# Recurrence stage: where the dense products stand between the levels, and who makes the exclusive sums

## The reference, cut to what matters

```python
def hgrn2_direction(q, i, z, lb, qc, ic, zc, ctx_out, reverse):
    kc, lfc = forget_terms(zc, lb)
    ...
    k, lf = forget_terms(z, lb)
    o, _ = hgrn2_scan(flip(q), flip(k), flip(i), flip(lf), s_ctx, True)
    ...
step (per chunk):
    scores = jnp.einsum('bhcd,bhsd,bhcsd->bhcs', q_n, k_n, w)
    o_n = o_inter + jnp.einsum('bhcs,bhse->bhce', scores, v_n)
    return d_n[..., None] * s + jnp.einsum('bhcd,bhce->bhde', ks_n, v_n), o_n
```

## Time and profile before

| | before |
|---|---|
| median of the runs (3) | 2460.62 us |
| lowest, highest | 2453.39 us, 2463.84 us |
| the profiled execution | 2457.86 us, span 2456.1 us |
| TensorE busy in the span | 2243.3 us (91%) |
| VectorE, GpSimd, ScalarE busy | 1104.9 us, 835.7 us, 668.0 us |
| mean granted TensorE clock | 0.948 |

### The profile page before, as it was taken

How to read it: one execution, slowest core, us unless ns; L and a number is a source line. 1 busy time by engine, 2 the same in 40 slices (tenths; PEclk the granted TensorE clock), 3 DMA queues, 4 the chain that set the end, 5 groups by cost and what they waited for, 6 DMA issues and landing times. The chain is left out here.

```text
span 2456.1 us, 27907 instructions
## 1 busy us (share of the span) xinstructions
PE 2243.3 (91%) x11655; PEld 1798.7 (73%) x11655; DVE 1104.9 (45%) x1647; ACT 668.0 (27%) x1030; POOL 835.7 (34%) x393
## 2 busy tenths in 40 slices
PE   5989996978999999999798878999998999999998
PEld 3768885856676767787665667888887767888886
DVE  2023557652556556556996553111116783111113
ACT  3222223223444444453111333010003163010111
POOL 1322102410323323223800024554554345454553
PEclk7999997979999999999899988999999999999999
DMA  9321115351101011112121012332322222232322
GB/s 296 83 72 52 35 35 172 79 163 52 35 23 47 18 35 35 35 52 78 42 65 35 35 35 70 102 103 86 103 92 97 86 86 69 86 103 88 101 95 77
DMA packets 173212, 187.45 MB, mean 76 GB/s; under 512 B 25552, under 2 KB 151840, under 8 KB 172960
## 3 DMA queue, kind: packets, MB, share of 16 engines
q1 hardware_dynamic: 165520, 178.56, 23.1%
q10 hardware_dynamic: 6992, 5.01, 0.7%
q0 software_dynamic: 576, 2.10, 0.2%
HBM read 183.56 MB, written 2.10 MB: 76 GB/s over the span
## 5 line engine op out<-in xcount | busy, mean ns | idle before, releaser
L2816 POOL TENSOR_TENSOR weights_lo<-weights_raw,weights_hi 128x2048 fp32r<-128x2048 f32 (+1 forms) x104 | 471.0, 4528 | 849.5 <-ACT weights_hi L1334 637.6
L646 PE MATMUL ring<-input_hi,weights_hi 128*128 128x512 f32 x784 | 305.4, 390 | 0.0
L648 PE MATMUL ring<-input_hi,weights_lo 128*128 128x512 f32 x784 | 305.0, 389 | 0.0
L647 PE MATMUL ring<-input_lo,weights_hi 128*128 128x512 f32 x784 | 305.0, 389 | 0.0
L2653 DVE CAST weights_hi<-weights_raw 128x2048 fp32r<-128x2048 f32 (+1 forms) x72 | 88.8, 1233 | 378.6 <-PE ring L648 173.9
L2807 POOL TENSOR_TENSOR h_w<-h_p 128x512 f32<-128x512 f32 x56 | 70.3, 1256 | 448.1 <-PE ring L935 367.6
L908 PE MATMUL obank<-acts,weights_raw 128*128 128x512 f32 x384 | 175.2, 611 | 0.8 <-issue 0.8
L646 PEld LDWEIGHTS ring<-input_hi,weights_hi 128*128 128x128 f32 x784 | 147.2, 188 | 31.1 <-issue 0.5
L648 PEld LDWEIGHTS ring<-input_hi,weights_lo 128*128 128x128 f32 x784 | 147.2, 188 | 30.6
L647 PEld LDWEIGHTS ring<-input_lo,weights_hi 128*128 128x128 f32 x784 | 147.2, 188 | 30.5 <-issue 0.2
L919 PE MATMUL obank<-weights_raw,acts 128*128 128x256 f32 x640 | 145.4, 387 | 0.0
(11 more groups left out here) (457 smaller groups left out, 4459.2 us busy)
## 6 DMA issues: line engine op xcount, KB each, us to landing
weights_raw<-in_w_ada SPq DMA_DIRECT2D x24, 1024.0 KB, 7.2
weights_raw<-in_ffn_w_gate SPq DMA_DIRECT2D x22, 1024.0 KB, 5.2
weights_raw<-in_ffn_w_up SPq DMA_DIRECT2D x22, 1024.0 KB, 5.2
weights_raw<-in_w_in_c SPq DMA_DIRECT2D x20, 1024.0 KB, 5.1
weights_raw<-in_ffn_w_down SPq DMA_DIRECT2D x16, 1024.0 KB, 4.9
weights_raw<-in_w_in_ab SPq DMA_DIRECT2D x9, 1024.0 KB, 5.2
weights_raw<-in_ev_w_in SPq DMA_DIRECT2D x8, 1024.0 KB, 5.8
weights_raw<-in_od_w_in SPq DMA_DIRECT2D x8, 1024.0 KB, 5.8
```

The costliest lines, as they stand in the source:

```text
L646: pe.matmul(o, hi[:, k, ms], xh[:, k, t0:t0 + n], start=k == 0, stop=False)
L647: pe.matmul(o, hi[:, k, ms], xl[:, k, t0:t0 + n], start=False, stop=False)
L648: last = pe.matmul(o, lo[:, k, ms], xh[:, k, t0:t0 + n], start=False, stop=k == KD - 1)
L2816: pool.tensor_tensor(W_LO[slot][:, 0:kt, :], WR[:, slot, 0:kt, :], w_hi[:, 0:kt, :], ALU.subtract).then_inc(sem("w_lo"), 1)
```

## The change

There are four edits.

1. `c_slots`: units of the dense product are put behind other levels. Steps with five units (0, 2, 4) now have them behind levels 0, 1, 2, 4 and in a place 7 behind level 6; steps with six (1, 3, 5, 6) behind 0, 1, 2, 3, 5 and in place 7. Step 7 is as before. ScalarE's evictions move along.
2. For backward steps the scans start at the second token and add the neighbour's term, which gives sums without the token's own term. The chunk sums add that term back (12 elements). GpSimd's `exclusive` and ScalarE's wait for it are gone. Two small fills of the first column are new, in the preparation of step 1 alone.
3. The query's part of `state_operands` becomes `query_operand`, behind `level_scores(st, 0)` and the previous pair's `inside`, ahead of `states`.
4. Ahead of step 0, `state_factors(0)` and the first two level exponentials stand in front of ScalarE's evictions of the second and third i unit.

```diff
@@ c_slots
-            return units + [None] * (8 - len(units))
+            places = range(8) if st == LAST else (0, 1, 2, 4, 7) if len(units) == 5 else (0, 1, 2, 3, 5, 7)
+            placed = dict(zip(places, units))
+            return [placed.get(i) for i in range(8)]
@@ ScalarE, state_factors
                 if d:
-                    act.wait_ge(sem("hg_excl"), STEPS[st][0] + 1)
                     act.activation(HZ[b][:, :, :], HP[b][:, :, :], ACT.Exp)
@@ ScalarE, ahead of step 0
-            for part in range(3):
-                take_product(("i", 0, part))
+            take_product(("i", 0, 0))
             state_factors(0)
             level_exp(0)
             level_exp(1)
+            take_product(("i", 0, 1))
+            take_product(("i", 0, 2))
@@ VectorE, log_f_and_sums, backward steps
+                    for h in range(HH):
+                        dve.tensor_tensor_scan(HP[b][:, h, 1:L], HT_[b][:, h, 0:L - 1], tab("chunk", 1, L), 0.0, ALU.add, ALU.mult)
+                        last = dve.tensor_tensor_scan(HP[b][:, h, L + 1:LT], HT_[b][:, h, L:LT - 1], tab("chunk", 1, LC), 0.0, ALU.add, ALU.mult)
+                    link(last)
+                    link(dve.tensor_tensor(PL[b], ends[0], ends[1], ALU.add))
@@ VectorE
             def state_operands(st):
...
+            def query_operand(st):
+
+                b, q = st % 2, STEPS[st][0] % 2
                 dve.wait_ge(*product_emptied(("q", STEPS[st][0], 1)))
                 dve.tensor_tensor(HT_[b][:, :, 0:L], HT_[b][:, :, 0:L], HQ[q][:, :, :], ALU.mult).then_inc(sem("hg_qi"), 1)
@@ GpSimd
-            def exclusive(st):
-
-                b, d = st % 2, STEPS[st][1]
-                if d == 1:
-                    pool.wait_ge(sem("hg_sums"), st + 1)
-                    pool.tensor_tensor(HP[b][:, :, :], HP[b][:, :, :], HT_[b][:, :, :], ALU.subtract).then_inc(sem("hg_excl"), 1)
```

More of the change, by code:

```diff
@@ L2113, in log_f_and_sums @@
                 dve.wait_ge(sem("hg_lf"), st + 1)
[L2114 to L2118, removed]
+                ends = [v[:, :, :].rearrange("p h (c t) -> p h c t", t=P)[:, :, :, P - 1] for v in (HP[b], HT_[b])]
+                if STEPS[st][1] == 0:
+                    for h in range(HH):
+                        dve.tensor_tensor_scan(HP[b][:, h, 0:L], tab("chunk"), HT_[b][:, h, 0:L], 0.0, ALU.mult, ALU.add)
+                        last = dve.tensor_tensor_scan(HP[b][:, h, L:LT], tab("chunk", 0, LC), HT_[b][:, h, L:LT], 0.0, ALU.mult, ALU.add)
+                    link(last)
+                    link(dve.tensor_copy(PL[b], ends[0]))
+                else:
+                    if st == 1:
+                        dve.memset(HP[b][:, :, 0:1], 0.0)
+                        link(dve.memset(HP[b][:, :, L:L + 1], 0.0))
+                    for h in range(HH):
+                        dve.tensor_tensor_scan(HP[b][:, h, 1:L], HT_[b][:, h, 0:L - 1], tab("chunk", 1, L), 0.0, ALU.add, ALU.mult)
+                        last = dve.tensor_tensor_scan(HP[b][:, h, L + 1:LT], HT_[b][:, h, L:LT - 1], tab("chunk", 1, LC), 0.0, ALU.add, ALU.mult)
+                    link(last)
+                    link(dve.tensor_tensor(PL[b], ends[0], ends[1], ALU.add))
                 dve.tensor_copy(DEC[b], PL[b]).then_inc(sem("hg_sums"), 1)
             def state_operands(st):
-                b, q = st % 2, STEPS[st][0] % 2
+                b = st % 2
                 dve.wait_ge(sem("hg_k"), st + 1)
@@ L2251, in _ @@
                 more = st + 1 < len(STEPS)
+                dve.wait_ge(*product_emptied(("q", hb, 1)))
                 level_operand(7 * st)
@@ L2257, in _ @@
                     inside(hb - 1)
+                query_operand(st)
                 states(st)
@@ L2787, in _ @@
         def _(pool):
-            def exclusive(st):
-                b, d = st % 2, STEPS[st][1]
-                if d == 1:
-                    pool.wait_ge(sem("hg_sums"), st + 1)
-                    pool.tensor_tensor(HP[b][:, :, :], HP[b][:, :, :], HT_[b][:, :, :], ALU.subtract).then_inc(sem("hg_excl"), 1)
-                    pool.wait_ge(sem("hg_excl"), STEPS[st][0] + 1)
             def level_args(g):
@@ L2845, in _ @@
                     if more:
-                        exclusive(st + 1)
                         pool.wait_ge(sem("hg_sums"), st + 2)
```

## The result

The changed kernel takes 2465.58 us (median of 20 runs, 2463.21 to 2468.83) against 2459.59 us before (20 runs, 2451.96 to 2463.84): ratio 1.0033, interval 1.0026 to 1.0041. It is 6 us slower; 2467 was forecast. The profiled execution took 2463.21 us, its span 2461.4.

A forecast was written before the change was run, and what follows sets the result against it. TensorE was taken to bound the kernel, through its idle time and clock. Steps 0 to 6 gave +17.4 us, the start -8.9, step 7 -1.7: together +6.8, forecast 2467 us, range 2450 to 2482.

The forecast's parts named there:

- The start: Step 0: with factors made ahead of two evictions, level 0 starts at about 604.3 instead of 613.18, -8.9 us.
- The step ends: Seven step ends: with a unit behind level 6, level 0 waits about 0.4 us instead of 1.65 to 2.1.
- Level 4 in even steps: Steps 0, 2, 4: without the unit before it, TensorE waits 4.5 us for the operand, three times, 13.5 us.
- Level 5 in odd steps and step 6: Without the unit before it, TensorE waits 5.85 us for the operand, four times, 23.4 us.
- The clock: Behind each of the seven new waits TensorE's low clock costs d = 3.0 us, bounds 0 and 5.0.
- Rivals B: Waits as worked out, but the clock hardly falls, 0 to 1.7 us per wait: 2451 to 2458 us; chance 0.18.
- C: Long low-clock stretches behind the waits at levels 4 and 5, 5 us each: 2481 us; chance 0.14.
- Rival D: Step-end waits shrink, but the clock still falls at all seven, 1.8 us each: 2480 us; chance 0.09.
- The rule of the Trainium skill: Transposes don't count as busy for the clock, so turned keys would still lower it at step ends; weighed against the forecast.
- Edit 2: Level 5's operand without GpSimd's subtraction: second half 0.69 us instead of 3.91; the wait would be hidden without edit 1.
- Edit 3: Query's operand moved ahead of the states and level 2's operand: worth nothing, both ways; 1.2 us in three steps if open.
- Rival E: VectorE's chain to the levels' operands gets shorter, 1.7 us in each of seven steps: 2446 us; chance 0.09.

The follow-up runs named there:

- the start alone: Edit 4 alone on the kernel before (first factors and exponentials ahead of two evictions): 2450.22 us, ratio 0.9969.
- the fillers: Changed kernel with 4 filler matmuls ahead of level 4 and 6 ahead of level 5 at the seven waits: 2452.98 us, ratio to before 0.9973.
- the old places: Changed kernel with the dense product's units back where they stood before (edits 2, 3 and 4): 2439.92 us, ratio to before 0.9929.
- the sums alone: Edit 2 alone on the kernel before (exclusive sums by the scan, no subtraction on GpSimd): 2459.68 us, ratio 1.0008.
- the query back: Changed kernel with the query's operand back in its old place (edits 1, 2, 4): 2467.13 us, ratio to before 1.0034.

## Why the prediction was right, point by point

**The start**, -8.9: level 0 at 604.48 instead of 613.18, -8.7. Right, and confirmed by the start alone.

**The step ends**, seven of 0.4 us: 0.32 each.

**Level 4 in even steps**, 4.5 us: 4.34, three times. **Level 5 in odd steps and step 6**, 5.85 us: 5.83 three times and 6.13 in step 6. The sum of the seven, 36.9 us: 36.6. (The numbers given for the odd steps, 724.6 - 718.66, make 5.9 and not 5.85, which is 0.3 us in all.) Both came out of one comparison: where TensorE could be without the unit, and when VectorE's operand is ready in the trace of before.

**The clock**, d = 3.0 us: 472.86 us of the seven steps (level 0 at 604.48 to level 0 at 1077.34), less 411.3 of work, 36.6 and 2.3 of waits, leave 22.7 us, 3.2 each; the fillers gave 2.9. It can also be counted wait by wait, from the start of the level behind it to the end of the unit, against the same two groups at full clock: 3.5, 3.1, 2.9, 2.8, 2.7, 2.7 and 4.2 us in steps 0 to 6, 21.8 together. Each of these is half of the low stretch that lies behind its wait (7.0, 6.2, 5.7, 5.6, 5.4, 5.4 and 8.4 us; the rest of the stretch lies inside the wait, in all seven). So the mean was right, while a single wait costs anything from 2.7 to 4.2. The stretch behind a wait was foreseen; that the clock falls inside the wait was not, and it is why the mean clock of the stage reads 0.94, the lowest value that the prediction allowed, where 7 x 3.0 us in 472.0 would make 0.96. Rivals B (none or little) and C (5.0) are out. Rival D is out: level 0 takes 1.97 us after each of the seven step ends, with turned keys right ahead of it, and step 7's clock is 0.99 instead of 0.97. The rule of the Trainium skill that was weighed, on transposes ("TensorE: Matmul & The Clock Gate", "Part 4: PE-mode transpose"), made nothing visible here. A stretch of the kernel before speaks against it more plainly than the earlier trace rows: from 533.49 to 539.33 TensorE does nothing but transposes (32 instructions of L688), and in their midst the granted clock rises from 0.50 (536 to 537) over 0.82 (537 to 538) to 1.00.

**Edit 2.** The operand's second half takes 0.68 us instead of 3.91, and in step 0 VectorE ends it at 651.0. That part was right. The sentence that without edit 1 the wait "would be hidden" was right only for level 5: the runs with the old places and with the sums alone show that the time came up again at the turned keys, 7.5 us in three waits. The prediction's sum did not rest on it, since the unit at the step's end covers that too.

**Edit 3**, nothing: right within the change (the query back, 1.5 us within the scatter), but not by itself, where it is some 4 us.

**Rival E**, shorter chains: out, 36.6 us is what the old chain gives.

**What was off, and what was luck:** the effect in the stage is +7.4 us, +6.8 was forecast; the median moved by 6.0. By parts: the start -8.9, steps 0 to 6 +18.2 (forecast +17.4), step 7 to the stage's end -1.9 (forecast -1.7). That it came out so close is in part luck. The 22.7 us of low clock before, and with them the 411.3 us of work, rest on a mean clock read as 0.95, which leaves 2.3 us either way; counted group by group the low clock cost 22.0. And d was the mean of two waits of another stage. The later stages of the profiled execution are 2.3 us shorter, which no part of the change explains; they scatter by -2.3 to +3.5 us over the kernels here.

## What to carry to other kernels

Work between two dependent pieces is cover, and what it covers is read by setting two times of the trace side by side: when the engine would arrive without it, and when the operand is ready. Moving it from a 4 to 6 us gap to a 1.7 us gap loses both the difference and the clock behind it; the unit with the least behind it (here the one behind level 5) is the one to move. A wait that ends last in a view is not the longest chain: taking it away can just bring out the next one, so follow the chain to the end of the step before booking the gain.

## What the runs showed of the hardware

Seven idle times of 4.3 to 6.1 us in front of full work each cost about 3 us more by the clock (2.7 to 4.2), and filling most of their length with matmuls that nobody reads took that away (clock 1.00 over 457 us). The clock had already fallen to 0.50 while TensorE stood, about 1.1 us into the wait at level 4 of step 0 and 1.8 us into that at level 5 of step 1; how much of the low stretch falls on work, and so what a wait costs, depends on that. Keeping the array busy in this way made the changed kernel 12.6 us faster, although no operand came earlier; where a wait can't be covered by useful work, this is a cheap half of the remedy. Instructions of VectorE with two inputs in SBUF take longer beside GpSimd's own: level 4's operand halves take 1.53 and 1.52 us beside `level_args`, and halves of the same shape 0.68 where GpSimd is idle.
